# The mLSTM gates projected first and worked out between gemm units, with the modulation sums hosted by other groups

## The reference

```python
mod = silu(c) @ w_mod + b_mod          # six vectors of 2048: sh1, sc1, ga1, sh2, sc2, ga2
p = modulate(rmsnorm(x), sh1, sc1) @ w_in   # columns: mlstm q, k, v, o, gates (32), diff q, k, v
# mlstm: q, k through a 3-tap depthwise conv and silu; per head and direction
#   i, f gates -> log-sigmoid, cumulative sums, running maxima -> chunk weights
m = mlstm(q, k, v, i, f) normed, times g_mlstm, times sigmoid(o)
d = diff_attend(rope(q), rope(k), v) normed, times g_diff
x = x + ga1 * rmsnorm(concat(m, d) @ w_out)
x = x + ga2 * rmsnorm(conv_ffn(modulate(rmsnorm(x), sh2, sc2)))
```

## Time and profile before

| | |
|---|---|
| median of 3 runs | 3,517.84 us (3,506.66 to 3,519.39) |
| the profiled execution, its time | 3,516.11 us |
| its span, first to last instruction | 3,514.3 us |
| mean granted clock of PE | 0.933 |
| PE busy | 3,070.4 us, 87% |
| DVE busy | 2,223.7 us, 63% |
| ACT busy | 1,209.6 us, 34% |
| POOL busy | 132.5 us, 4% |
| bytes moved | 589.20 MB, mean 168 GB/s |

### The profile page before, as it was taken

One profiled execution on the slowest core, in us unless ns is written; L12 is line 12 of the kernel. 1 busy time (PEld: TensorE's weight loads), 2 busy tenths in 40 slices (PEclk: granted clock), 3 DMA queues, 4 the chain that ended last, 5 costly groups with the idle time before them and its releaser, 6 DMA issues. The chain is left out here.

```text
span 3514.3 us, 41974 instructions
## 1 busy us (share of the span) xinstructions
PE 3070.4 (87%) x16281; PEld 2536.6 (72%) x16281; DVE 2223.7 (63%) x3193; ACT 1209.6 (34%) x1747; POOL 132.5 (4%) x198
## 2 busy tenths in 40 slices
PE   5999788986769999998996999888998979978996
PEld 2587486766659999997885888766766767956665
DVE  5766674657657778876875668845347845584354
ACT  6631332222444444333334222124242133324242
POOL 1000000001010000000001000000000000000000
PEclk9999999997889999999998999989998989989998
DMA  8865054750446766666774556520205626561333
GB/s 258 295 231 180 1 174 140 259 204 1 162 138 222 251 223 217 235 214 222 264 262 129 195 169 198 173 91 25 82 26 186 206 100 205 180 207 56 103 120 102
DMA packets 255286, 589.20 MB, mean 168 GB/s; under 512 B 21945, under 2 KB 30369, under 8 KB 250480
## 3 DMA queue, kind: packets, MB, share of 16 engines
q1 hardware_dynamic: 245760, 544.54, 46.7%
q0 software_dynamic: 8928, 41.32, 3.3%
q10 hardware_dynamic: 400, 0.66, 0.1%
HBM read 571.72 MB, written 14.72 MB: 167 GB/s over the span
## 5 line engine op out<-in xcount | busy, mean ns | idle before, releaser
L2224 ACT ACTIVATE w_hi<-raw 128x1024 fp32r<-128x1024 f32 (+2 forms) x732 | 742.3, 1032 | 1402.1 <-PE bank L2295 813.9
L2245 DVE TENSOR_TENSOR w_lo<-raw,w_hi 128x1024 fp32r<-128x1024 f32 (+2 forms) x732 | 859.1, 1190 | 550.1 <-ACT w_hi L2224 547.4
L625 DVE SCALAR_TENSOR_TENSOR acc<-raw,sc_t,acc 128x1024 f32<-128x1024 f32 x480 | 601.0, 1279 | 42.5 <-DMA acc<-in_b_ada 32.8
L2293 PE MATMUL bank<-w_hi,l_hT_hi 128*128 128x512 f32 (+1 forms) x1056 | 398.8, 378 | 46.5 <-DVE w_lo L2245 45.9
L2303 PE MATMUL bank<-f_hT_hi,w_hi 128*128 128x256 f32 x1408 | 408.5, 290 | 29.3 <-DVE w_lo L2245 29.0
L2304 PE MATMUL bank<-f_hT_lo,w_hi 128*128 128x256 f32 x1408 | 406.1, 288 | 0.0
L2305 PE MATMUL bank<-f_hT_hi,w_lo 128*128 128x256 f32 x1408 | 405.9, 288 | 0.0
L2294 PE MATMUL bank<-w_lo,l_hT_hi 128*128 128x512 f32 (+1 forms) x1056 | 395.2, 374 | 0.0
L2295 PE MATMUL bank<-w_hi,l_hT_lo 128*128 128x512 f32 (+1 forms) x1056 | 394.7, 374 | 0.0
L2303 PEld LDWEIGHTS bank<-f_hT_hi,w_hi 128*128 128x128 f32 x1408 | 278.4, 198 | 33.9 <-DVE w_lo L2245 31.6
L2304 PEld LDWEIGHTS bank<-f_hT_lo,w_hi 128*128 128x128 f32 x1408 | 278.6, 198 | 0.0
(11 more groups left out here) (435 smaller groups left out, 4654.4 us busy)
## 6 DMA issues: line engine op xcount, KB each, us to landing
raw<-in_w_in SPq DMA_DIRECT2D x240, 512.0 KB, 4.8
raw<-in_w_mod SPq DMA_DIRECT2D x192, 512.0 KB, 5.1
raw<-in_w_ada SPq DMA_DIRECT2D x192, 512.0 KB, 4.4
raw<-in_w_up SPq DMA_DIRECT2D x176, 512.0 KB, 5.1
raw<-in_w_out SPq DMA_DIRECT2D x96, 512.0 KB, 4.6
raw<-in_w_down SPq DMA_DIRECT2D x88, 512.0 KB, 5.3
raw<-in_w_in SPq DMA_DIRECT2D x32, 288.0 KB, 3.2
raw<-in_w_ukv SPq DMA_DIRECT2D x16, 512.0 KB, 4.5
```

Source lines behind the costliest of these rows:

```text
L625: e.scalar_tensor_tensor(acc[a][:, :], raw[s % RAW_SLOTS][:, :], scalar, acc[a][:, :], ALU.mult, ALU.add).then_inc(fma_done, 1)
L2224: e.activation(slot(w_hi[u % SPLIT_SLOTS], g.width), slot(raw[s % RAW_SLOTS], g.width), ACT.Copy).then_inc(hi_ready, 1)
L2245: e.tensor_tensor(slot(w_lo[u % SPLIT_SLOTS], g.width), slot(raw[s % RAW_SLOTS], g.width), slot(w_hi[u % SPLIT_SLOTS], g.width).bitcast(F3 ...
L2293: e.matmul(o, xh[:, k, tok], hi[:, kk, :], start=first, stop=False)
```

## The change

The 32 gate columns (mg) are projected as the first group of the second phase, and mg is evacuated at the very next step instead of five later (`soon`). The order of the groups is mg, mk0, mo0, mk1, mo1, mq0, mq1, mv0, mv1. The gate stage and one barrier are gone: its work is cut into hooks at steps of mk0, mo0 and mk1, on PE banks that the group then running does not use, with two waits of PE (`gates_free_pe`) before those banks are written by a later group. Its tiles lie elsewhere; Mrow is copied to M_rows at the start of the chunk stage. onehot and g_mlstm are loaded by POOL at the start of the chunk stage, and the two products of mo with g_mlstm are done by POOL in the chunk stage ahead of items 6 and 10. The sums are hosted otherwise: `gemms` takes a list of hosts, a start and a length in main units. The first phase hosts three sums (two of sums_mix and the first of sums_ffn, whose turn comes after the last unit), the second phase the next two, the w_out phase the last one. The norms of the diff heads start after mk1 instead of mq0. A place can have several hooks.

```diff
-                leave = min(turn + SUM_LEAVE_AFTER, end) if g.kind == "F" else min(at + LEAVE_AFTER, end)
+                leave = min(turn + SUM_LEAVE_AFTER, end) if g.kind == "F" else min(at + (1 if g.soon else LEAVE_AFTER), end)
...
-        def gemms(mains, sums=(), lead=8, tail=3, rest=4, side=None, first=None, then=None, start=(), hooks=None):
+        def gemms(mains, sums=(), lead=8, tail=3, rest=4, side=None, first=None, then=None, start=(), hooks=None, hosts=None):
...
             room = (len(alone) - lead - tail) // max(len(sums), 1)
             hosted = {}
-            for i, m in enumerate(sums):
+            if hosts is None:
+                hosts = [(lead + i * room, room - rest) for i in range(len(sums))]
+            for (h0, hn), m in zip(hosts, sums):
                 for j in range(m.n_units):
-                    hosted.setdefault(lead + i * room + j * (room - rest) // m.n_units, []).append((m, j))
+                    hosted.setdefault(h0 + j * hn // m.n_units, []).append((m, j))
             steps, place_of = list(start), []
...
-                at = lead + i * room + (m.n_units - 1) * (room - rest) // m.n_units + 2
+                at = hosts[i][0] + (m.n_units - 1) * hosts[i][1] // m.n_units + 2
...
-        gemms([dq1, dk1] + gs[4:6], sums_mix, lead=8, side=(dk_group, drope_dve, 1), then=rows_out, start=start, hooks=hooks)
+        gemms([dq1, dk1] + gs[4:6], sums_mix + sums_ffn[0:1], hosts=[(8, 7), (15, 8), (23, 8)], side=(dk_group, drope_dve, 1), then=rows_out, start=start, hooks=hooks)
...
+        mg.soon = True
+        mk0, mo0, mk1, mo1 = mk_group(0), mo_group(0), mk_group(1), mo_group(1)
+        mq0, mq1 = mq_groups()
+        mv0, mv1 = mv_copy(0), mv_copy(1)
...
-        gemms(gs, sums_ffn, lead=16, side=(gs[0], diff_norms, 1), first=gd_pool)
...
-        def gates_pool(e):
-            aux_dmas(e, [(onehot[:, :, :], A["onehot"].rearrange("a (b c) -> a b c", b=HEADS))])
-            aux_dmas(e, [(gmb[:, :], A["g_mlstm"].broadcast_to([P, 1024]))])
-            e.memset(mv[:, :, :, HD:HD + 1], 1.0).then_inc(pool_order, 1)
-
-            e.wait_ge(aux_landed, n_aux_oh)
-            for t in range(2):
-                e.tensor_tensor(mo[:, t, :], mo[:, t, :], gmb[:, :], ALU.mult).then_inc(pool_order, 1)
...
+        def gates_turn_pe(e):
+            e.wait_ge(evac_act, mg.number + 1)
+            for t in range(4):
+                mm = e.transpose(banks[1][:, 32 * t:32 * t + 32], gT[:, P * t:P * t + P], ident[0:32, 0:32])
+            mm.then_inc(t_pe, 1)
...
+        def gates_log_act(e):
+            e.wait_ge(t_dve, g_dve + 1)
+            chain(e, "act", e.activation(lf[:, :, :], la[:, :, :], ACT.Exp, scale=-1.0))
+            e.activation(lf[:, :, :], lf[:, :, :], ACT.Ln, bias=1.0).then_inc(t_act, 1)
...
+        def gates_rows_pe(e):
+            e.wait_ge(t_dve, g_dve + 2)
+            for d in range(2):
+                for t in range(4):
+                    e.matmul(banks[d][0:HEADS, P * t:P * t + P], la[:, 2 * t + d, :], tri[d], start=True, stop=True)
+                    mm = e.transpose(banks[2 + d][0:HEADS, P * t:P * t + P], iv[:, 2 * t + d, :], ident)
+            mm.then_inc(t_pe, 1)
...
+        def gates_scan(i):
+            sh = 1 << i
+            a_, b_ = (av[0][:, 0:2, :], av[1][:, 0:2, :]) if i == 0 else (cm[(i - 1) % 2][:, 0], cm[(i - 1) % 2][:, 1])
+            f, b = cm[i % 2][:, 0], cm[i % 2][:, 1]
+
+            def dve(e):
+                e.tensor_tensor(f[:, :, sh:P], a_[:, :, sh:P], a_[:, :, 0:P - sh], ALU.max)
+                e.tensor_copy(f[:, :, 0:sh], a_[:, :, 0:sh])
+                e.tensor_tensor(b[:, :, 0:P - sh], b_[:, :, 0:P - sh], b_[:, :, sh:P], ALU.max)
+                chain(e, "dve", e.tensor_copy(b[:, :, P - sh:P], b_[:, :, P - sh:P]))
+            return dve
+
...
-        stage(pool=gates_pool, dve=gates_dve, act=gates_act, pe=gates_pe)
...
+        def gates_free_pe(n):
+            def pe(e):
+                e.wait_ge(t_dve, g_dve + n)
+            return pe
+
+        def gates_hooks(steps):
+            hooks = {"pe": {}, "act": {}, "dve": {}, "pool": {}}
+            at = lambda g, j: steps.index((g, j))
+            hook(hooks, "pe", at(mk0, 1), gates_turn_pe)
+            hook(hooks, "dve", at(mk0, 2), gates_bias_dve)
+            hook(hooks, "act", at(mk0, 3), gates_log_act)
+            hook(hooks, "dve", at(mk0, 4), gates_log_dve)
+            hook(hooks, "pe", at(mk0, 4), gates_rows_pe)
+            hook(hooks, "dve", at(mk0, 5), gates_rows_dve)
+            for i in range(7):
+                hook(hooks, "dve", at(mk0, 6) if i < 3 else at(mk0, 7) if i < 5 else at(mo0, 0), gates_scan(i))
+            hook(hooks, "pe", at(mo0, 0), gates_free_pe(3))
+            hook(hooks, "dve", at(mk1, 2), gates_state_dve)
+            hook(hooks, "act", at(mk1, 4), gates_exp_act)
+            hook(hooks, "dve", at(mk1, 5), gates_diag_dve)
+            hook(hooks, "pe", at(mk1, 6), gates_cols_pe)
+            hook(hooks, "dve", at(mk1, 7), gates_cols_dve)
+            hook(hooks, "pe", at(mq1, 0), gates_free_pe(7))
+            return hooks
+
+        gemms([mg, mk0, mo0, mk1, mo1, mq0, mq1, mv0, mv1], sums_ffn[1:3], hosts=[(26, 28), (56, 9)],
+              side=(mk1, diff_norms, 1), first=gd_pool, hooks=gates_hooks)
+        n_aux_oh = aux_total(1)
+        n_aux_gm = aux_total(1)
...
+            e.wait_ge(t_act, g_act + 3)
...
-                    mm = e.matmul(gates[:, 256 + P * j:256 + P * j + P], onehot[:, h, :], Mrow[:, d, t, :], start=True, stop=True)
+                    mm = e.matmul(gates[:, 256 + P * j:256 + P * j + P], onehot[:, h, :], M_rows[:, d, t, :], start=True, stop=True)
...
+            e.activation(M_rows[:, :, :, :], Mrow[:, :, :, :], ACT.Copy).then_inc(t_act, 1)
...
         def m_pool(e):
+            aux_dmas(e, [(onehot[:, :, :], A["onehot"].rearrange("a (b c) -> a b c", b=HEADS))])
+            e.memset(mv[:, :, :, HD:HD + 1], 1.0).then_inc(pool_order, 1)
+            e.wait_ge(aux_landed, n_aux_oh)
+            aux_dmas(e, [(gmb[:, :], A["g_mlstm"].broadcast_to([P, 1024]))])
             for i in range(NCH):
                 d = i % 2
+                if i in (6, 10):
+                    e.wait_ge(aux_landed, n_aux_gm)
+                    e.tensor_tensor(mo[:, i // 8, :], mo[:, i // 8, :], gmb[:, :], ALU.mult)
                 e.wait_ge(m_act_a, i + 1)
                 e.tensor_tensor(Em[:, i % 2], Em[:, i % 2], tri[d].unsqueeze(1).broadcast_to([P, 2, P]),
                                 ALU.mult).then_inc(m_pool_a, 1)
...
-                      lambda t, q=q: y1[:, t, 512 * q:512 * q + 512]) for q in range(4)], first=res1)
+                      lambda t, q=q: y1[:, t, 512 * q:512 * q + 512]) for q in range(4)],
+              sums_ffn[3:4], hosts=[(3, 22)], first=res1)
...
-                if at in hooks:
-                    hooks[at](e)
+                for hook in hooks.get(at, []):
+                    hook(e)
```

More of the change, by code:

```diff
@@ L111, in __init__ @@
         self.number = None
+        self.soon = False
         self.banks_from = None
@@ L354, in gemms @@
             number_units(steps)
+            if callable(hooks):
+                hooks = hooks(steps)
             program.append(("gemms", None, Phase(steps, side, first, then, hooks or {})))
@@ L1216, in build, with hook @@
         ends = [start.index((mods[2 * q + 1], 7)) for q in range(4)]
-        hooks = {"pe": {}, "act": {0: start_squares}, "dve": {1: start_rsqrt}, "pool": {}}
+        hooks = {"pe": {}, "act": {}, "dve": {}, "pool": {}}
+        def hook(hooks, who, at, what):
+            hooks[who].setdefault(at, []).append(what)
+        hook(hooks, "act", 0, start_squares)
+        hook(hooks, "dve", 1, start_rsqrt)
         for t in range(4):
-            hooks["dve"][2 + t] = start_scale(t)
+            hook(hooks, "dve", 2 + t, start_scale(t))
         for at, k0, k1 in ((7, 0, 6), (11, 6, 12), (15, 12, 16)):
-            hooks["pe"][at] = start_turn(k0, k1)
+            hook(hooks, "pe", at, start_turn(k0, k1))
             for k in range(k0, k1, 2):
-                hooks["act"][at + 2 + (k - k0) // 2] = start_copy(k)
+                hook(hooks, "act", at + 2 + (k - k0) // 2, start_copy(k))
         def start_last(part):
@@ L1494, in gates_act, with gates_diag_dve, gates_cols_pe @@
             last.then_inc(t_act, 1)
-        def gates_pe(e):
-            for t in range(4):
-                mm = e.transpose(banks[6][:, 32 * t:32 * t + 32], gT[:, P * t:P * t + P], ident[0:32, 0:32])
-            mm.then_inc(t_pe, 1)
-            e.wait_ge(t_dve, g_dve + 2)
+        def gates_diag_dve(e):
+            e.wait_ge(t_act, g_act + 2)
             for d in range(2):
-                for t in range(4):
-                    e.matmul(banks[d][0:HEADS, P * t:P * t + P], la[:, 2 * t + d, :], tri[d], start=True, stop=True)
-                    mm = e.transpose(banks[2 + d][0:HEADS, P * t:P * t + P], iv[:, 2 * t + d, :], ident)
-            mm.then_inc(t_pe, 1)
```

(4 more changed lines are left out.)

134 lines of the change are left out of this document (63 added, 71 removed).

## The result

The kernel after takes 3,491.97 us (median of 4 runs, 3,488.95 to 3,495.53) against 3,514.93 us of before (4 runs beside it): a ratio of 0.9938, 95% interval 0.9915 to 0.9961, 23 us less. A second comparison gave 3,495.33 against 3,516.30 us, the same ratio (0.9919 to 0.9957). The forecast was 3,487 in a range of 3,472 to 3,503.

The account below looks back on a forecast made before the run. PE was taken to bound the gemm phases, with a dependent chain in the gate stage. -29.4 + 3.5 + 5 - 10 + 1.7 = -29.2 us, from 3,516.1 to 3,487 us, range 3,472 to 3,503.

Parts of the forecast that it names:

- The gate stage: Between second phase and chunk stage: 32.3 us go, 2.9 return waiting for onehot; gain 29.4 us (28 to 31).
- The chain is hidden: Gate chain's DVE steps in mk0 and mk1 cost nothing; rival, chance 0.05: up to 14 us return, 3,501, 3,515 with ACT's.
- The second phase: From 453.65 to 773.95 us: stalls and extras 33.5 against 44.0 us, taken as -10 (-15 to 0).
- the forecast's five stalls: PE waits in the second phase, before mk0.0, after mo0.3, at mo1.2, within mo1, at mq0/mq1: 3.0, 1.5, 5.5, 4.1, 1.9 us.
- The first phase: Sixteen more F units in dv0 and dv1, longer stalls after dk1, and ffn0's turn standing alone: +5 us (2 to 9).
- The product on POOL: Chunk stage: mo times g_mlstm between POOL's masks makes DVE wait; +3.5 us, between 0 and 4.7.
- One sign that I gave: Chunk stage: the operation that stands for L1675 would twice take 2 us or more.
- w_out: w_out phase: 16 F units, 22 us of DVE over 22 units, hidden; only their own turn shows, +1.7 us (1 to 4).
- The rest: Everything behind w_out, the same instructions in both kernels: no change, 0 us.
- the ring gives nothing back: Rival, chance 0.18: DVE's queue tighter or clock falls again; second phase 0 instead of -10, first costs 9: 3,501 us.
- the clock's: Rival, chance 0.03: granted clock stays at 0.50 through mk0 and mo0, doubling their 65 us of PE: 3,552 us.
- The better case: Chance 0.08: no port conflict in chunk stage (-3.5), no clock loss at mg bubble (-2.8), side work falls well: 3,478 us.

Follow-up runs that it names:

- the hosting alone: The kernel before with only the new sharing-out of the sums (three, two, one), keeping its own group order and gate stage; 3,510.31 us, before 3,515.32.

## Why the prediction was right, and where it was not

- **The gate stage**, -29.4: measured -29.6. The wait for onehot was taken at 2.9 us from its neighbour's landing; the gap is 3.9 as a whole, with the evacuation of mv1's 1.3 us in it.
- **The chain is hidden**: shown for DVE and ACT. PE has no idle time at the hooks, and the scans done twice cost nothing. That rival is out. PE's own part was never hidden: 6.6 in the forecast, 5.8 measured.
- **The second phase**, -10: measured -11.3, and the forecast's five stalls are those of the trace: at mk0.0 3.0 against 2.88, at the end of mk0's cover 1.5 against 1.69, at mo1.2 5.5 against 5.72, within mo1 4.1 against 3.17, behind mq0 1.9 against 2.03. The clock loss after the first was put at 2.8; unit mk0.0 took 7.3 us instead of 5.6, 1.7. Two things beneath the sum were less good: the hosting alone is worth -26.0 and the new order and chain take back about 15 of it, which I had as a smaller gain and a smaller loss. That the two errors met is luck. (The 6.0 us for mo0 in the list of before is 6.4 by its own figures, 28 - 21.6; it changes nothing.)
- **The first phase**, +5 (2 to 9): measured +7.6 up to attention, with the 3 us of spread said above. Its stalls are 3.41, 1.66 and 1.72 us where 3.8, 1.9 and 1.1 were expected, so the terms hold and the 2.6 us over are not assigned. Attention gave 1.6 us back: the second phase now opens with mg, whose splits are 64 columns wide, 0.63 us for four, so PE waits there 1.12 us and not 2.93. I had not counted that.
- **The product on POOL**, +3.5: measured 3.5 by leaving it out, with the mechanism of the lock; 5.1 in the second trace of the same kernel, so the exact hit is partly luck. One sign that I gave came only in part: in this trace L1738 is at 2 us or more once, not twice, since the second product met L1745; in the second trace of the kernel it is twice at 2.27. The chunk stage as a whole is only 1.7 longer, since its first items ran at a clock of 0.82 instead of 0.73 and took 1.8 us less. No term of the sum had that.
- **w_out**, "1.2 + 1.0 a unit, hidden; its own turn shows: +1.7 (1 to 4)": this is the step that failed, by 8.0 us. I costed the F units' time on DVE and the turn, and not what an F group needs before its first unit: the accumulator's bias load, a DMA on POOL's queue, behind 3 MB of others. In the second phase the same load has only g_diff's ahead of it and 26 units of lead; here it has two to three units. With the load first w_out is 89.6, +2.3.
- **The rest**, 0: measured -2.9, without a change in its instructions, and another 4.5 us apart in a second trace of the same kernel. It is no effect of the change.

From the forecast to the result: first phase +2.6, attention -1.6, second phase -1.3, gap -0.2, chunk stage -1.8, w_out +8.0, rest -2.9, together +2.8 of span. The total was close partly because errors of both signs met; the w_out term alone lay outside its bounds. Of the rivals, "the ring gives nothing back" is refuted (-11.3), and so is the clock's: PE had 0.97 in the second phase. The better case is out too: the port conflict came, and so did a clock loss after mg.

## What to carry to other kernels

When work is moved to a new host, list everything it needs before its first instruction, its small loads above all, and what stands ahead of them in that queue at the new place: a 4 KB load behind 3 MB cost here three times what the hosted work itself did. A dependent chain of small operations can be cut into hooks between long units: here its pieces on DVE and ACT cost nothing, its matmuls on PE 5.8 us. The order of groups that it forces costs as well, so evacuations should still meet long units. A product on POOL was not free beside a DVE that is on the critical path, at either of the two places tried in that stretch. And a term that comes out right in one trace can hide two that don't: cut a stage again, at events inside it, before its number is believed.

## What the runs showed of the hardware that was not expected

- A 4 KB load on POOL's queue took 10.9 us from issue to landing behind 2 MB and 1 MB of the same queue, 1.8 us ahead of them. By their issues and times to landing, the three landed at 891.7, 895.0 and 895.3 us, in the order of issue. The Trainium skill (DMA: Bandwidth & Descriptors, Two DMAs through the same engine are not ordered) says that within one queue of one DMA engine descriptors start in order; the rows agree, and the small load pays for it.
- A DVE operation on 128x2 with two SBUF inputs took 2.26 us instead of 0.16, since POOL had begun a product 0.1 us earlier; 0.63 us beside a mask, as in the earlier trace rows. A reciprocal with one tensor input, begun 0.09 us after the second product, took its usual 0.17.
- The part behind w_out, with the same instructions and data, took from 2,504.5 to 2,514.6 us over the profiled executions, 0.4%, and the chunk stage 108.2 and 109.4 us in two traces of one kernel. In the chunk stage the granted clock goes with it: the same five intervals took 21.8 us at 0.82 and 23.6 at 0.73. What drives the clock there, and the spread of the rest, was not looked into.
- Splitting the products into smaller pieces, or loading onehot before mv1 ends, was not tried.
